# The first norm's rows turned by a diagonal of reciprocals, with three clock matmuls ahead in each layer

## The reference

```python
def rmsnorm(x, g):
    y = x * lax.rsqrt(jnp.mean(x * x, axis=-1, keepdims=True) + EPS)
    return y * g

for l in range(2):
    u = rmsnorm(x, norm_mix_g[l])              # the first norm
    proj = u @ w_in[l]                         # 1024 -> 3072, split among three head groups
    mix = concat(out_lru, out_conv, out_retention) @ w_out[l]
    x = x + mix
    x = x + hier_moe(rmsnorm(x, norm_ffn_g[l]), ...)   # the second norm; 32 experts, top 2
y = rmsnorm(x, final_norm_g)
```

## Time and profile before

| | |
|---|---|
| median of 3 executions | 859.84 us (858.94 to 861.62) |
| the profiled execution, time | 859.28 us |
| its span, first to last instruction | 857.5 us |
| TensorE busy | 822.5 us, 96% |
| TensorE weight loads | 464.1 us, 54% |
| VectorE busy | 478.6 us, 56% |
| ScalarE busy | 176.5 us, 21% |
| GpSimd busy | 140.5 us, 16% |
| DMA | 260.11 MB, mean 303 GB/s |

### The profile page before, as it was taken

The page is one execution under the profiler, slowest core; times in us unless marked ns, Lnnn a source line. Parts: engine busy times, 40 slices in busy tenths (PEclk is TensorE's granted clock), DMA queues, the critical chain, the costliest instruction groups (busy, mean ns, idle before and its releaser), DMA issues.

```text
span 857.5 us, 13544 instructions
## 1 busy us (share of the span) xinstructions
PE 822.5 (96%) x5282; PEld 464.1 (54%) x5282; DVE 478.6 (56%) x1099; ACT 176.5 (21%) x361; POOL 140.5 (16%) x193
## 2 busy tenths in 40 slices
PE   7999999989998899999999999999999979999995
PEld 5664554676555455455366545447655545545552
DVE  3397787263112377775546977953521215777666
ACT  3213122301221111111321221232022111111113
POOL 0030031011212223221000300300121113213120
PEclk9999999999999999999999999999999999999999
DMA  9942973869999999999960348358599999999951
GB/s 309 315 159 109 373 208 74 291 217 407 419 414 376 414 416 402 414 415 408 367 255 0 148 170 223 103 165 336 220 413 416 416 414 417 412 402 414 414 235 56
DMA packets 93531, 260.11 MB, mean 303 GB/s; under 512 B 34265, under 2 KB 43629, under 8 KB 77531
## 3 DMA queue, kind: packets, MB, share of 16 engines
q1 hardware_dynamic: 83994, 247.00, 75.6%
q0 software_dynamic: 7680, 9.39, 3.2%
q10 hardware_dynamic: 1792, 2.84, 0.9%
HBM read 265.22 MB, written 15.18 MB: 327 GB/s over the span
## 4 chain that ended last, share of the span: by engine, by line
PE 82%; DMA 8%; DVE 4%; issue 3%; SPq 2%; ACT 1%; POOL 0%; DVEq 0%; POOLq 0%; ACTq 0%
PE psum L1120 23%; PE psum L788 12%; PE psum L1143 12%; PE psum L728 7%; PE psum L797 7%; PE psum L986 5%; DMA rows<-xn_scratch,sg 4%; PE psum L1172 3%; DMA ring<-in_moe_w 3%; PE psum L1166 2%; PE psum L807 2%; DMA ring<-in_w_in 1%; PE psum L1157 1%; PE psum L1027 1%; PE psum L863 1%
## 5 line engine op out<-in xcount | busy, mean ns | idle before, releaser
L1120 PE MATMUL psum<-ring,arena 128*64 128x256 f32 x1920 | 220.4, 382 | 5.3 <-issue 4.1
L1120 PEld LDWEIGHTS psum<-ring,arena 128*64 128x64 f32 x1920 | 135.6, 137 | 75.6 <-issue 14.7
L1143 PE MATMUL psum<-ring,arena 128*64 128x512 f32 x480 | 117.8, 603 | 5.8 <-issue 5.8
L788 PE MATMUL psum<-ring,uT 128*128 128x512 f32 x256 | 114.3, 599 | 0.5 <-DVE uT L1354 0.4
L1861 DVE TENSOR_TENSOR arena<-psum,gff 128x512 f32<-128x512 f32 x64 | 43.6, 687 | 68.1 <-PE psum L728 68.1
L788 PEld LDWEIGHTS psum<-ring,uT 128*128 128x128 f32 x256 | 47.9, 191 | 55.4 <-issue 54.4
L1869 DVE SCALAR_TENSOR_TENSOR arena<-arena,psum 128x128 f32<-128x128 f32 x64 | 18.2, 285 | 104.3 <-ACT arena L2199 90.7
L1915 DVE TENSOR_TENSOR x<-x,psum 128x512 f32<-128x512 f32 x80 | 51.5, 684 | 41.3 <-PE psum L1172 35.6
L2180 ACT ACTIVATE arena<-psum,sg 128x512 f32<-128x512 f32 x64 | 44.0, 687 | 121.0 <-PE psum L1143 119.2
L1143 PEld LDWEIGHTS psum<-ring,arena 128*64 128x64 f32 x480 | 35.6, 138 | 60.4 <-issue 59.1
L797 PE MATMUL psum<-uT,ring 128*128 128x288 f32 x256 | 63.8, 407 | 0.8 <-DMA ring<-in_w_in 0.8
(11 more groups left out here) (326 smaller groups left out, 941.1 us busy)
## 6 DMA issues: line engine op xcount, KB each, us to landing
ring<-in_moe_w SPq DMA_DIRECT2D x180, 1024.0 KB, 17.9
ring<-in_w_in SPq DMA_DIRECT2D x24, 1024.0 KB, 14.2
ring<-in_w_out SPq DMA_DIRECT2D x8, 1024.0 KB, 7.3
y_scratch<-in_w_out SPq DMA_DIRECT2D x1, 2304.0 KB, 19.1
arena<-in_state_ret SPq DMA_DIRECT2D x16, 128.0 KB, 6.1
out<-arena SPq DMA_DIRECT2D x16, 128.0 KB, 2.5
xn_scratch<-rows ACTq DMA_DIRECT2D x4, 512.0 KB, 4.6
uT<-in_moe_w SPq DMA_DIRECT2D x2, 1024.0 KB, 8.2
```

Of the source, the lines that this page charges most:

```text
L788: i = pe.matmul(b, uTk[:, k, 128 * t:128 * t + 128], w[:, k, :], start=k == 0, stop=k == KT - 1)
L1120: i = pe.matmul(b[64 * j:64 * j + 64, 0:FE], xsT[:, u // 2, k, s], weight13(e, j, k), start=k == 0, stop=k == KT - 1, skip_group_check=True)
L1143: i = pe.matmul(b[64 * q:64 * q + 64, :], hT[:, q, f, :], weight2(4 * it + 2 * pair + q, f, j), start=f == 0, stop=f == 1, skip_group_chec ...
```

## The change

The first norm's rows are turned unscaled, straight from x; the reciprocals enter in the turning itself. DVE now builds a diagonal: the identity times the row's reciprocal, n by n (128 columns, or 32 for tile 2), in the first columns of the same `rows` buffer. TensorE takes x's columns as weights and streams that diagonal in an ordinary float32 matmul, where it streamed the identity in transpose mode. The second norm stays a transpose. DVE's queue waits once for the identity's DMA, ahead of its first tile. The clock matmuls go from 6 and 5 to 3 in each layer.

```diff
-WAIT_NORM, WAIT_CHOICE, WAIT_MARKS, WAIT_GATES, WAIT_ROWS = (6, 5), 16, 6, 7, 7
+WAIT_NORM, WAIT_CHOICE, WAIT_MARKS, WAIT_GATES, WAIT_ROWS = (3, 3), 16, 6, 7, 7
...
+                scale = ident[0:n, 0:n] if s else rows[0:n, t % 2, 0:n]
                 if s:
 
                     for name in ((f"w{t}0", f"w{t}1") if t < 2 else ("w2",)):
                         freed(pe, l, name)
-                    r = x[0:n, t, :].rearrange("p (m k) -> p m k", k=KT)
                 else:
                     pe.wait_ge(rows_ready, norm_turn(l, s, t))
-                    r = rows[0:n, t % 2, :].rearrange("p (m k) -> p m k", k=KT)
+                r = x[0:n, t, :].rearrange("p (m k) -> p m k", k=KT)
...
-                        i = transpose(b[:, k - k0, :], r[:, :, k], n)
+                        i = pe.transpose(b[:, k - k0, :], r[:, :, k], scale) if s else pe.matmul(
+                            b[:, k - k0, :], r[:, :, k], scale, start=True, stop=True, skip_group_check=True)
...
-                S(rows[0:n, t % 2, :], x[0:n, t, :], rec[0:n, t:t + 1], None, ALU.mult).then_inc(rows_ready, 1)
+                S(rows[0:n, t % 2, 0:n], C("ident", n)[:, 0:n], rec[0:n, t:t + 1], None, ALU.mult).then_inc(rows_ready, 1)
...
                     dve.wait_ge(g_in, 16)
+                    dve.wait_ge(ident_in, 16)
                     first_tile(l)
```

## The result

The changed kernel takes 876.5 us (median of 6, 873.6 to 878.1) where the kernel before took 861.1 in the same session: the ratio is 1.0196 (95% interval 1.0172 to 1.0219), 2% slower. The forecast was +2.1 us with a range that ended at +4.2. The profiled execution, 878.1 us, is the longest of the six.

A forecast was written before the change was run, and what follows sets the result against it. TensorE was taken to bound the kernel, with work in 96% of the span. Layer 0's +0.42 and layer 1's +1.69 us made +2.1 us, forecast from the 859.84 us median as 861.9 us, range 860.3 to 864.0.

The forecast's parts named there:

- What bounds the kernel: Whole kernel: TensorE has work in 96% of the span; a delay of the mixers passes on one for one.
- 16 records of 8: First norm's tiles: a float32 matmul leaves two records, a transpose one, so a tile's 8 become 16.
- What a record costs: First norm: matmul or transpose records cost the same, 0.112 us (lower clock 0.213); a tile gains 0.88 us (1.71).
- The rival of four transposes: First norm's tiles: a float32 matmul costs four transposes; more than +9 us, 869 us; chance 0.02.
- DVE's product: L1345, ahead of each first-norm tile: 128 columns take 0.24 us, bounds 0.17 and 0.41, where 1024 took 0.75.
- The free wait for the identity: DVE's queue, layer 0's first tile: the added wait for the identity's DMA costs nothing.
- the rise of the clock: Layer 0, in q0: the clock rises at about 10.88 us and stays there, so q0 ends 0.3 us later.
- the sign of being wrong by the rise: Layer 0: the forecast is wrong if the clock's rise is off by over 1 us.
- The two waits of layer 0: Layer 0: waits for parameter rows and a w_in granule leave +0.42 of 2.05 us.
- the two meet: Layer 1, first tile: DVE's product and the six clock records end together, 429.48 and 429.50, using up both savings.
- the rival had it rise later: Layer 0: the clock rises later, after a hole between clock matmuls and first turned row; +3.8, 863.7 us; chance 0.15.
- the dearest rival that kept 0.11 us a record: Layer 0: the clock rises later, costing 1.7 us that nothing absorbs; +3.8, 863.7 us; chance 0.15.

The follow-up runs named there:

- the run with dense filler: The kernel before with dense clock matmuls added ahead of five of the first norm's tiles, 13 or 8 each: 870.6 us against 860.4, ratio 1.0136.

## Why the prediction was wrong, step by step

- *What bounds the kernel*, and that a delay passes on one for one: right, by the run with dense filler.
- *16 records of 8*: right. *What a record costs*: here it failed. "Real matmul or transpose, 128 rows or 32, a record costs the same" joined two rows of which neither was the case in hand: the earlier trace rows has plain matmuls with neighbouring weight columns, has spread columns in transpose mode. The changed line has plain matmuls with spread columns, and no row of before had that. It asked for a bound from both sides, and I gave one value. The term was 0.88 us for a tile at the upper level and measured 2.8 to 2.9 (16 x 0.239 against 8 x 0.11). Five tiles were short by about 2 us each, 10 of the 16.8 us by which the profiled execution (+18.9) missed the sum (+2.1); the two falls are 4.6 and the rest of the layers 2.3.
- *The rival of four transposes* had 0.02, on the ground that the clock line refuted it. In effect it was the nearest: a turned block of 128 columns took 2 x 0.239 = 0.48 us against 0.110, 4.3 times. The Trainium skill's "four times" (TensorE: Matmul & The Clock Gate, Terms) thus fits the strided case here and, with 128 columns to stream, not the neighbouring one (2.0 times); with 32 columns neighbouring ones give 2 x 0.113 against 0.066, 3.4 times. The rival was also priced too low, with four tiles at the upper level: there are five, and 5 x 2.6 less the waits' 1.6 is 11.6 us or more, 871 us.
- *DVE's product* at 0.24 us: 0.28 measured, in the bounds. The free wait for the identity: right. The first tile of layer 0 stood at 6.59 and q0 at 10.59 where I had 6.73 and 10.30 (the clock matmuls, too, began 0.14 sooner); the rise of the clock was where I left it (q0's second record at 11.17, as from 10.9), so tile 0 added 0.45 us and not 0.3. That the rise was there is luck: it moves by more than 1 us between executions with the same front, so the sign of being wrong by the rise could not have told anything.
- *The two waits of layer 0* swallowed 1.6 us, as the sum had it; with more behind them they were simply used up.
- *Layer 1*: "the two meet" was right for the start (438.55, 0.34 us behind the start of DVE's product; 0.30 forecast), but q0 waited for 16 slow records and came 1.85 us late, not 0.07 early.
- *The clock*: the rival had it rise later, which did not happen in the changed kernel's profile; early and late rise are less rivals than two draws of one spread (8.4 to 12.5 us). It fell instead, at tile 2, for 6.8 and 3.4 us. I had read "the clock is up" as settled once TensorE's line is unbroken; nothing in the sum asked what an unbroken line of such records does.
- *The range* ended at the dearest rival that kept 0.11 us a record. The one case beyond it was the one that the records were said to "all but refute".

## What to carry to other kernels

Turn with a transpose, not with a float32 matmul: the matmul takes two records, and four times as long when the weights are read with a step of four elements or more. If a diagonal has to be folded into the turn, take the features in neighbouring blocks and load the next weights (and the gains, which these runs left in their old order) in the same order; it still costs two records for one, +2 us here. A spread weight operand is harmless under a stream of 512 columns and dear under one of 128; a spread moving operand, 4 or more elements apart, is dear under both. When a cost is taken from two rows, ask whether either row has both properties of the new instruction.

## What the runs showed of the hardware

- Float32 operands of a plain matmul at the upper clock, 128 columns: 0.112, 0.118, 0.170, 0.233, 0.238 and 0.219 us a record at weight columns 1, 2, 3, 4, 8 and 16 elements apart; the moving operand 0.114 at 2, 0.226 at 4, 0.232 at 8. Transposes stay at 0.11 at 1, 8 and 16 when they stream 128 columns; with 32 columns they take 0.066 at 1 and 0.113 at 8. The Trainium skill says that SBUF is read in 16-byte lines and that two hits on a line are needed to hide its latency (Advanced Engine Details and Errata, SBUF Cachelines): two elements of 4 bytes at distance 2 share such a line and at distance 4 don't, which is where the step lies. Transposes are not exempt: their weight loads go from 137 to 198 ns (tile 2), the plain form's from 192 to 334. Why a plain load is the slower one at either distance stays open.
- The slow load takes 0.24 us at either level of the clock (0.240 in layer 0's first tile, 0.239 in layer 1), so at the lower level it costs only 0.03 us over the matmul's own 0.213.
- The granted clock can fall in a stretch in which TensorE never pauses (24.50 to 31.40 of the changed kernel, 6.90 of 6.90 us busy, 0.51). Single falls of 3.4 us, and one of 6.8 in the run with dense filler (window 188 to 196, 0.57), also came behind the mixers, at other places in each profile, the kernel before among them; I did not trace those to a part of the change.
- The first rise of the clock lay anywhere from 8.4 to 12.5 us in eleven profiles, at 9.2, 10.9 and 11.0 in three with the same front, and once in the middle of transposes.
